# Thirty-two unused bytes ahead of the activations' buffers in a two-block transformer kernel

## The reference

```python
m = hgrn2_mixer(rmsnorm(x, norm_pre_mix[i]), hgrn_w_in[j], hgrn_w_out[j], ...)
x = x + rmsnorm(m, norm_post_mix[i])
x = x + rmsnorm(conv_ffn(rmsnorm(x, norm_pre_ffn[i]), ffn_w_in[i], ...), norm_post_ffn[i])
...
proj = rmsnorm_2(x, mix_norm[l]) @ w_in[l]        # attention and delta rule
x = x + mixed @ w_out[l]
x = x + memory_cross_attention(rmsnorm_2(x, xattn_norm[l]), mem_n, ...)
x = x + conv_ffn_2(rmsnorm_2(x, ffn_norm[l]), w_up[l], ...)   # 2048 -> 2 x 5632 -> 2048
return rmsnorm_2(x, final_norm)
```

## Time and profile before

| | us |
|---|---|
| median of three runs | 2696.8 |
| the three runs | 2696.35 to 2698.36 |
| the profiled execution | 2697.01 |
| its span, first to last instruction | 2695.2 |
| TensorE busy | 2683.5 |
| VectorE busy | 1971.6 |
| ScalarE busy | 1335.3 |
| GpSimd busy | 133.9 |

### The profile page before, as it was taken

How to read it: one execution, slowest core, us unless ns; L and a number is a source line. 1 busy time by engine, 2 the same in 40 slices (tenths; PEclk the granted TensorE clock), 3 DMA queues, 4 the chain that set the end, 5 groups by cost and what they waited for, 6 DMA issues and landing times.

```text
span 2695.2 us, 47424 instructions
## 1 busy us (share of the span) xinstructions
PE 2683.5 (100%) x17616; PEld 2291.9 (85%) x17616; DVE 1971.6 (73%) x2721; ACT 1335.3 (50%) x1679; POOL 133.9 (5%) x138
## 2 busy tenths in 40 slices
PE   9999999999999999999999999999999999999998
PEld 8888888888888888888888888878888888888887
DVE  6888888878888888644466677767678888885444
ACT  6455555455444444433465566665644444443443
POOL 0211121210000000000000000000000000000000
PEclk9999999999999999999999999999999999999999
DMA  7555555475555555655645544355455555556554
GB/s 245 180 165 172 165 168 173 161 196 170 189 187 187 187 187 187 195 187 187 218 139 181 170 145 139 134 171 186 150 190 187 187 187 187 187 188 197 185 184 150
DMA packets 136197, 481.68 MB, mean 179 GB/s; under 512 B 14880, under 2 KB 19120, under 8 KB 135680
## 3 DMA queue, kind: packets, MB, share of 16 engines
q1 hardware_dynamic: 134160, 472.06, 53.2%
q0 software_dynamic: 1376, 7.46, 0.8%
q10 hardware_dynamic: 528, 0.26, 0.0%
HBM read 477.63 MB, written 2.10 MB: 178 GB/s over the span
## 4 chain that ended last, share of the span: by engine, by line
PE 82%; DVE 8%; issue 4%; DMA 3%; ACT 2%; DVEq 1%; SPq 0%; ACTq 0%
PE acc L442 29%; PE acc L444 15%; PE acc L465 8%; PE acc L467 8%; PE acc L466 8%; PE acc L414 4%; DMA raw<-stream 3%; DVE wts L362 3%; PE acc L415 2%; ACT wts L355 2%; DVE cy L2313 2%; DVE cin L392 1%; DVE half L380 1%; PE ps L1406 1%; PE ps L740 1%
## 5 line engine op out<-in xcount | busy, mean ns | idle before, releaser
L442 PE MATMUL acc<-hs,wts 128*128 128x512 f32 x4640 | 1626.8, 394 | 0.0
L362 DVE TENSOR_TENSOR wts<-raw,wts 128x1024 fp32r<-128x1024 f32 x888 | 1061.9, 1227 | 525.0 <-ACT wts L355 524.3
L355 ACT ACTIVATE wts<-raw 128x1024 fp32r<-128x1024 f32 x888 | 913.6, 1055 | 847.0 <-PE acc L444 367.9
L444 PE MATMUL acc<-hs,wts 128*128 128x256 f32 x4640 | 1297.1, 280 | 0.0
L442 PEld LDWEIGHTS acc<-hs,wts 128*128 128x128 f32 x4640 | 871.0, 188 | 194.1 <-DVE wts L362 0.9
L444 PEld LDWEIGHTS acc<-hs,wts 128*128 128x128 f32 x4640 | 871.5, 188 | 0.5
L467 PE MATMUL acc<-wts,acts 128*128 128x512 f32 x688 | 272.8, 396 | 0.0
L465 PE MATMUL acc<-wts,acts 128*128 128x512 f32 x688 | 272.6, 396 | 0.2 <-DVE wts L362 0.2
L466 PE MATMUL acc<-wts,acts 128*128 128x512 f32 x688 | 270.4, 393 | 0.0
L369 ACT ACTIVATE half<-acc 128x512 f32<-128x512 f32 x161 | 95.3, 592 | 157.7 <-PE acc L444 138.9
L466 PEld LDWEIGHTS acc<-wts,acts 128*128 128x128 f32 x688 | 129.2, 188 | 32.2
(11 more groups left out here) (361 smaller groups left out, 2172.7 us busy)
## 6 DMA issues: line engine op xcount, KB each, us to landing
raw<-stream SPq DMA_DIRECT2D x888, 512.0 KB, 4.1
xf<-xT SPq DMA_DIRECT2D x8, 256.0 KB, 6.6
raw<-stream SPq DMA_DIRECT2D x8, 256.0 KB, 6.7
fm<-memT POOLq DMA_DIRECT2D x2, 1024.0 KB, 6.6
fw<-stream POOLq DMA_DIRECT2D x2, 1024.0 KB, 10.7
memr<-memT POOLq DMA_DIRECT2D x1, 2048.0 KB, 9.8
outT<-memr SPq DMA_DIRECT2D x7, 256.0 KB, 2.8
KQ<-masks POOLq DMA_DIRECT2D x1, 448.0 KB, 5.7
```

The lines of the kernel that those rows point to most:

```text
L355: nc.scalar.activation(high, source, ACT.Copy).then_inc(hi_ready, 1)
L362: nc.vector.tensor_tensor(low, source, high.bitcast(F32), ALU.subtract).then_inc(lo_ready, 1)
L442: nc.tensor.matmul(acc[:, 2 * par + n, :], whi[:, b, c:c + P], src[:, kt, :], start=start, stop=False)
L444: mm = nc.tensor.matmul(acc[:, 2 * par + n, 0:T], wlo[:, b, c:c + P], src[:, kt, 0:T], start=False, stop=stop)
```

## The change

One name is added behind `kept`, with eight floats in each partition, which makes 32 bytes. Nothing reads or writes it. It stays allocated for the whole kernel, so everything that is named later lies 32 bytes higher. The highest address in use was 228704, in a partition of 229376 bytes.

```diff
@@ -141,6 +141,7 @@
         lnr = kept[:, 1]
         lb, oml = (kept[:, 0, a:a + 2 * HEADS].rearrange("p (a b) -> p a b", a=2) for a in (0, 2 * HEADS))
         ident, ones, row_ge, row_le = (cst[:, c, :] for c in range(4))
+        sb("to_line", [P, 8])
 
         with ExitStack() as st:
             hs = sb("hs", [P, DT, 2 * T], F32R, st)
```

## The result

| | before | after |
|---|---|---|
| median, us | 2696.6 (2696.3 to 2698.4, 4 runs) | 2713.0 (2712.2 to 2714.0, 4 runs) |
| profiled execution and its span | 2697.0, 2695.2 | 2712.5, 2710.7 |

The ratio is 1.0059, interval 1.0047 to 1.0071. That is slower by more than the 0.2% that a measurement of this kernel tells from no change, and the forecast was no change. I read the profile after in the order of before: first the page. The instructions are as many as in the earlier trace rows and the clock is as full, but PE is busy for 2699.8 us where it was 2683.5.

What follows compares the result with a forecast made beforehand. PE was taken to bound the kernel, busy 2683.5 us of a span of 2695.2. The sum was 2697.0 + 0 (VectorE, ScalarE) + 0 (DMA) + 0 (PE) = 2697.0 us, range 2677 to 2714.

Steps and rivals of the forecast that it cites:

- rival C: Features, lines 442 and 444: a moving operand at 0 is slower, pair 0.3466 to 0.3500, 2713.0 us; chance 0.19.
- all three streams: PE's main matmuls: features (activations move), tokens and wide (weights move); effect taken as 0, bounds from 3.4 ns a pair.
- (a): Lines 2053, 2056 and 1465 beside feature pairs: other stationary start, same moving start, same pitch, so effect 0.
- (c): Line 927, fp32 matmuls with both starts at 32: 0.216 us for 256 columns, so 32 alone doesn't slow PE.
- the four combinations of remainders by 64: Moving/stationary starts by 64 bytes on PE: 32/0 (features), 0/32 (tokens, wide), 32/32 (line 1465), and 0/0 after the change.
- Rival A: Tokens and wide: a stationary start at 32 costs something, so 8.0 us off, 2689.0 us; chance 0.28.
- Rivals B and D: PE streams: B, both misaligned starts cost, 2673.0 us, chance 0.08; D, misalignment costs the whole 8%, 2498.4, chance 0.03.
- The 8%: Excess of features, tokens and wide over one column a cycle on PE, 8 to 9%, 198.6 us.
- The gap formula behind the 2532 us: Warm matmul gap of N/2.4 + 2.5 ns on PE: streams at 325 and 215.8 ns, kernel an estimated 2532 us.

Runs made afterwards that it cites:

- all256: Kernel before with 64 unused floats (256 bytes) in place of the change's 8: 2697.7 us, ratio 0.9999.
- cols: Computation left out, matmul streams alone by stationary width and moving columns, start differences 0 and 32: 226.7 and 234.4 ns for 512 columns, 128 wide.
- w32h32: Kernel before with 32 bytes ahead of wts (the weights) and 32 behind it: 2712.4 us, ratio 1.0061.
- acts96: Kernel before with 96 bytes behind hold, moving the wide streams' activations while hs stays: 2679.0 us, ratio 0.9937.
- w32h0: Kernel before with 32 bytes ahead of wts (the weights), 32 behind it, and the change's 32 too: 2709.8 us, ratio 1.0052.
- map2: Computation left out, streams alone over finer starts, feature streams behind one, two and three short matmuls: 0.348, 0.348, 0.354 us a pair at difference 224.
- acts0: Kernel before with 32 bytes behind hold, moving the wide streams' activations while hs stays: 2685.9 us, ratio 0.9959.

## Why the prediction of no change was wrong

The measured 2713.0 lies inside the stated range of 2677 to 2714, at its very end, because that end was chosen to take in rival C, which had a chance of 0.19. What was forecast, no change at 2697, did not come.

- *PE is the only part that can show; VectorE, ScalarE and DMA take 0.* Right. `cy<-cin` has a median of 478 ns after 480, `cin` 692 after 693, the transfers 6.4 and 6.5 us after 6.6 and 6.7, and all256 moves every buffer and costs nothing.
- *Nothing covers PE, so a change of pitch shows in full.* Right in kind: +27.3 and -11.8 us in the stages make the span's +15.5. Pitch times count would give 4704 x 6.7 = +31.5 and 2976 x 4.4 = -13.1. Matmuls at a stream's beginning or beside small ones did not change, and in the first up-projection before has some ten stretches of ten pairs at 352 to 360 ns a pair, where after has none once the stream has begun.
- *"I take 0 for all three streams."* This is the step that failed. (a) tested one start at a time, and where it had one matmul of another kind inside feature pairs its rows resolve 0.01 us in 0.23, while the whole effect is 2 to 5 ns a matmul. It also read a single matmul, and the pitch belongs to a stream. (c) was about float32 and said nothing of fp32r: cols has float32 at 216 ns for either start. (Its "two cycles" a column are those of one of the two records that each float32 matmul leaves.) Most of all, the four combinations of remainders by 64 were the wrong table. Before and after differ in the difference of the two operands, 160 and 192 by 256, and this combination was not in it.
- *Rival C, 2713.0.* Its place and its sign were right, its time agrees by chance. It had the pair go from 0.3466 to 0.3500, and it went to 0.3533, twice as far; it had the others stay, and wide gave 4.4 ns a matmul back. Two errors of 11 to 12 us each cancelled: features cost 27.3 where it had 16.0, and wide gave 11.8 where it had nothing. Its mechanism, a moving operand at 0, is refuted by w32h32 (moving at 32, 353.3 ns) and by wide in acts96 (moving at 0, 226.7 ns, the quickest of all).
- *Rival A.* Half of what it would show did: wide fell, even below its 0.231. But features paid more than wide gave, and its mechanism fails: in w32h0 the stationary operand of wide starts at 0, and wide stays at 233.3.
- *Rivals B and D.* No combination brought features below 346.7 or wide below 226.7. The 8% is not a price of misalignment; the best start takes a third of it off wide, (233.3 - 226.7) / (233.3 - 213.3). The gap formula behind the 2532 us is stated in the Trainium skill (TensorE: Matmul & The Clock Gate, Back-to-back issue gap) for an isolated matmul, so it was no forecast for streams; no fp32r stream here came nearer to its 215.8 ns than 226.7.
- *The Trainium skill's rule.* SBUF — State Buffer, Specifications, has 16-byte cachelines and a penalty for each access that crosses to a new one. All starts here are multiples of 32 bytes, and the pitch differs by up to 3%, so the measurement decides: the rule does not tell which starts are quick. By it the time would have been 2697.0.

## What to carry to other kernels

Where PE is busy without gaps, read the pitch of each kind of stream to the nanosecond before and after anything that moves a buffer, even an unused name: a busy share of 100% hides 3%. For fp32r streams choose the start of the activations by its difference from the weights' (here 0 by 256 bytes for wide, 32 or 160 for features), and choose it per kind of stream, since one shift served them in opposite ways. A control that moves everything by 256 bytes tells a change in placement from one in work.

## What the runs showed of the hardware that I had not expected

- The pitch of 512 fp32r columns, weights moving, by the difference of the starts: 226.7 ns at 0, 228.9 at 192, 232.1 at 128, 233.3 to 234.2 elsewhere. Of a pair of 512 and 256, activations moving: 346.7 (32, 160), 350.0 (96), 351.0 to 351.3 (128) or 353.3 (192).
- The same instructions on the same addresses run at either 346.7 or 353.3 ns a pair at some differences (0, 224), and keep that pitch for hundreds of pairs in w32h0. In map2 only the number of short matmuls ahead of a stream differed. A pitch can also change inside a stream: wide in acts0 went from 228.9 to 233.3 ns.
- Narrower stationary operands, down to 32 columns, bring an fp32r matmul no closer to 213.3 ns (cols). At d = 0 the surplus over one column a cycle is the same 13.3 ns for 256, 384 and 512 moving columns.
